# Hybrid encoder layer in fp32: one rotary pass for all queries, and a first pair of tiles multiplied before its tokens are normalised

## The chip, the cores and the metric

One core of a Trainium2 chip (trn2) runs the whole layer in one launch. The metric is device time in microseconds of one execution. The kernel before took 926.9 us, the median of three runs (925.67 to 927.23).

## What is computed

One encoder layer over 1024 tokens of width 1024, all in float32:

```
h = rms_norm(x, g_pre)
proj = h @ w_in                      # 1024 -> 7424 columns
a_b, a_c, a_x, a_z, b_q, b_k, b_v, b_z, m_q, m_z, gate_logits = split(proj)
ya = short_gated_conv(a_b, a_c, a_x, w_conv) * silu(a_z)
q, k = partial_rope(b_q), partial_rope(b_k)       # 8 query heads, 2 key heads of 64; the first 16 dims turn
yb = window_attention_with_sink(q, k, b_v, sink) * silu(b_z)
ym = memory_cross_attention(m_q, mk, mv) * silu(m_z)
merged = gates[0]*(ya @ w_up_a) + gates[1]*(yb @ w_up_b) + gates[2]*(ym @ w_up_m)
out = x + rms_norm(merged @ w_out, g_post)
```

The kernel works on transposed activations: channels on partitions, the 1024 tokens along a row. The rotary turn is `t*cos + swapped(t)*sin` over rows; with 16 of 64 rows turning, cos is 1 and sin is 0 in the others.

## The kernel before, in words

Each fp32 operand is split in a high and a low part of type fp32r, and a product is three matmuls: high x high, high x low, low x high. For a weight block ACT makes the high part (`high_part`, L1207) and POOL the low part (`low_part`, L766) in one of the 4 slots of `ring`; the slots are numbered in the order in which TensorE uses them. So each slot has a place on ACT, then on POOL, then on TensorE, and ACT and POOL take them in order between whatever else stands there.

The projection runs in pairs of 128-column tiles. The first three pairs (key, four query tiles, value) are direct: 96 matmuls of 128x512 a pair. From pair 3 (`P_DIRECT`) on, each pair is one level of Strassen-Winograd: seven products P1, P2, P6, P7, P4, P5, P3 of 12 matmuls each, on 512x512 blocks of h and their combinations T3, T2, T4, T1. Attention begins in pair 4: `scores(0)` stands on TensorE ahead of P6 of pair 4 (L977).

**Start.** SP loads four blocks of x (L502), the identity, weights and the other four blocks. ACT squares (L1217), DVE makes the inverse roots and scales x, TensorE transposes (`turn_x`, L953, four transposes for one chunk of 128 channels and 512 tokens), ACT makes the high part of a chunk from PSUM (L1228), DVE or POOL the low part (L1583, L776), DVE or ACT a copy (L1587, L1233). `first_pair` then does six matmuls a chunk for pair 0, sixteen chunks (0 to 7 are the first 512 tokens). TensorE fills the waits before with small matmuls (`warm`, L1085).

**Rotary.** For each of the key tile and the four query tiles DVE shuffles rows (L1707), multiplies by cos (L1717, which frees the PSUM bank: `cos_made`), by sin (L1721) and adds (L1723): four instructions of 128x1024. ACT then makes the high part (L1284), POOL the low part (L787), and SP stores both in DRAM (`store_rope`, L492 to L498). Between them DVE makes the combinations of h (L1594, L1599, L1607, L1612) and their low parts (L1617), and the sums of weights (L1626 to L1643). `load_block(0)` (L548 to L553) reads the first query and key blocks back before `scores(0)`. The order on every engine is written out by hand.

Of the kernel before, what the change touches and what calls it, by code (L numbers as in the profile page):

```python
# [7 lines left out]
P = 128  # L8
D = 1024
SEQ = 1024  # L10
KC = D // P
# [39 lines left out]
WARM_STEPS = (28, 8, 4)  # L51

ROOT_GROUPS = (slice(0, 2), slice(2, 4), slice(4, NB))

POOL_CHUNKS = (2, 6, 8, 10, 12, 14)
# [56 lines left out]
COS0, SIN0, SWAP0, QHI0, VR0, VP0 = 4096, 5120, 6144, 0, 12288, 12288  # L112
ROTATED = (7168, 2048, 7168, 2048, 3072)
SWAPS = (SWAP0, SWAP0, SWAP0, VP0 + SEQ, SWAP0)
# [35 lines left out]
ROPES = [(0, None), (1, 0), (2, 1), (3, 2), (4, 3)]  # L150
# [29 lines left out]
SWAP_ROWS = [(r + ROT // 2) % ROT if r < ROT else r for r in range(HEAD // 2)]  # L180

# [23 lines left out]
def hybrid_layer(nc, x, mem, w8, wup, wmem, wout, g_pre, g_mem, g_post, w_conv, sink,  # L205
                 cos, sin, mask, ident_in, out):
    ctx = ExitStack()
    with ctx:
# [17 lines left out]
        hc = sb("hc", [P, 7, 2, HC, HALF], F32R)  # L226
# [13 lines left out]
        q_d = dram("q_d", (NB, P, 2, GROUP, P))  # L240
# [22 lines left out]
        rope_high_at = [f32r(at, SEQ) for at in (QHI0, QHI0 + SEQ, QHI0, QHI0 + SEQ, SWAP0)]  # L263
        rope_low_at = [f32r(at, SEQ) for at in ROTATED]
# [41 lines left out]
        def rotated(j):  # L306
            return f32(ROTATED[j], SEQ)

        def swap(j):
            return f32(SWAPS[j], SEQ)  # L310

# [36 lines left out]
        def sig_block(n):  # L348
            return f32(SIG0 + n % 2 * HALF, HALF)

        x_landed = [sem(f"x_landed{b}") for b in range(NB)]
        ident_landed, small_landed = sem("ident_landed"), sem("small_landed")
        spot_landed = [sem(f"spot_landed{j}") for j in range(4)]
        rope_landed, swapped, roped = sem("rope_landed"), sem("swapped"), sem("roped")
        rope_hi, rope_lo = sem("rope_hi"), sem("rope_lo")
        rope_stored = [sem(f"rope_stored{j}") for j in range(len(ROPES))]
# [3 lines left out]
        xs_pool = sem("xs_pool")  # L360
        x_turned, h_copied, h_copied_act, comb_hi = sem("x_turned"), sem("h_copied"), sem("h_copied_act"), sem("comb_hi")
# [5 lines left out]
        sum_made = {T3: sem("t3_made"), T2: sem("t2_made"), T4: sem("t4_made"), T1: sem("t1_made")}  # L367
# [10 lines left out]
        mem_landed, mem_ssq, mem_var, mem_root, memx_ready = (sem("mem_landed"), sem("mem_ssq"), sem("mem_var"),  # L378
                                                              sem("mem_root"), sem("memx_ready"))
# [20 lines left out]
        sq_made, out_var, out_root, out_ready = sem("sq_made"), sem("out_var"), sem("out_root"), sem("out_ready")  # L400
# [24 lines left out]
        def wait_stored(eng, j):  # L425
            eng.wait_ge(rope_stored[j], 16 * (6 if ROPES[j][1] is None else 4))

# [32 lines left out]
        def _(sp):  # L460
# [62 lines left out]
            for j in range(4):  # L523
                load_spot(j, 2)
# [1755 lines left out]
```

## Time and profile before

| | |
|---|---|
| median of 3 runs | 926.9 us |
| the profiled execution: its own time, its span | 925.96 us, 924.1 us |
| TensorE busy | 907.8 us (98%) |
| VectorE, ScalarE, GpSimd busy | 657.1, 439.2, 453.4 us |
| DMA | 126.56 MB, 137 GB/s mean |
| granted TensorE clock | 0.996 of full speed |

A time in what follows is counted from the start of the span. An instruction's duration overlaps that of the next on its engine, so the pace of an engine is read from start to start.

### The profile page before, as it was taken

Reading aid. Unit: us, or ns where it says so; the run is one execution under the profiler, and the core shown is the slowest. Engines: PE = TensorE matmul, PEld = TensorE weight load, DVE = VectorE, ACT = ScalarE, POOL = GpSimd, SP = SyncE. Lnnn points to the kernel's source line nnn. Section 1 sums busy time; section 2 is a strip of 40 time slices with the busy share of each in tenths; the row PEclk is TensorE's granted clock in tenths of the full one; section 3 lists DMA queues with packets and bytes.
Section 4 is the critical chain, followed back from the end, with each engine's and each line's share of the span. In section 5 each row is a group of like instructions: output and inputs, shape, how many; then the busy total and the mean of one; then the engine's idle time right before and its main releaser. Section 6 shows DMA issues by size and latency. Waiting matters only on the chain.

```text
span 924.1 us, 12763 instructions
## 1 busy us (share of the span) xinstructions
PE 907.8 (98%) x4376; PEld 763.3 (83%) x4376; DVE 657.1 (71%) x1060; ACT 439.2 (48%) x849; POOL 453.4 (49%) x303
## 2 busy tenths in 40 slices
PE   9999999999999999999999999999999999999995
PEld 8788788888888888888888888888888888888784
DVE  5689976565656566656576178888797358899887
ACT  7624464444444466544463434343444544445341
POOL 3546844444444444444446744444443636668452
PEclk9999999999999999999999999999999999999998
DMA  7243846252525242525255322222222974750333
GB/s 287 96 116 83 228 144 210 90 171 91 170 91 169 96 128 102 193 91 171 108 174 174 116 80 80 79 78 82 80 69 68 333 262 143 258 181 0 142 110 137
DMA packets 82336, 126.56 MB, mean 137 GB/s; under 512 B 7136, under 2 KB 40544, under 8 KB 82272
## 3 DMA queue, kind: packets, MB, share of 16 engines
q1 hardware_dynamic: 81952, 125.61, 41.2%
q8 instruction: 36, 0.59, 0.2%
q14 instruction: 28, 0.23, 0.1%
q10 hardware_dynamic: 320, 0.13, 0.1%
HBM read 92.56 MB, written 33.55 MB: 136 GB/s over the span
## 4 chain that ended last, share of the span: by engine, by line
PE 81%; DVE 8%; ACT 3%; DMA 3%; POOL 2%; issue 2%; SPq 1%; DVEq 0%; ACTq 0%
PE pm L866 17%; PE pm L864 17%; PE pm L865 17%; PE pm L1162 3%; PE pm L1163 3%; PE pm L1161 3%; PE pv L999 2%; PE sa L987 2%; PE sa L1163 2%; PE sa L1162 2%; PE sa L1161 2%; PE pv L1078 2%; PE sa L1058 1%; DVE area L2158 1%; DVE area L2135 1%
## 5 line engine op out<-in xcount | busy, mean ns | idle before, releaser
L766 POOL TENSOR_TENSOR ring<-spots,ring 128x512 fp32r<-128x512 f32 x234 | 340.9, 1460 | 389.9 <-ACT ring L1207 377.9
L864 PE MATMUL pm<-hc,ring 128*128 128x512 f32 x784 | 308.6, 394 | 0.0
L866 PE MATMUL pm<-hc,ring 128*128 128x512 f32 x784 | 305.8, 390 | 0.0
L865 PE MATMUL pm<-hc,ring 128*128 128x512 f32 x784 | 305.5, 390 | 0.0
L1207 ACT ACTIVATE ring<-spots 128x512 fp32r<-128x512 f32 x234 | 146.2, 628 | 268.6 <-PE pm L866 177.5
L866 PEld LDWEIGHTS pm<-hc,ring 128*128 128x128 f32 x784 | 147.2, 188 | 31.2
L864 PEld LDWEIGHTS pm<-hc,ring 128*128 128x128 f32 x784 | 147.3, 188 | 29.3 <-issue 0.6
L865 PEld LDWEIGHTS pm<-hc,ring 128*128 128x128 f32 x784 | 147.4, 188 | 28.9
L1161 PE MATMUL pm<-hc,ring 128*128 128x512 f32 x128 | 49.9, 390 | 0.0
L1162 PE MATMUL pm<-hc,ring 128*128 128x512 f32 x128 | 49.8, 389 | 0.0
L1163 PE MATMUL pm<-hc,ring 128*128 128x512 f32 x128 | 49.8, 389 | 0.0
L766 POOL TENSOR_TENSOR ring<-area,ring 128x512 fp32r<-128x512 f32 x28 | 41.6, 1484 | 12.2 <-ACT ring L1207 11.1
L1826 DVE TENSOR_TENSOR area<-pv,area 64x512 f32<-64x512 f32 x16 | 11.0, 689 | 49.1 <-ACT area L1334 49.1
L1664 DVE TENSOR_TENSOR snaps<-pm,snaps 128x512 f32<-128x512 f32 x26 | 17.9, 690 | 37.9 <-PE pm L866 37.8
L1457 ACT ACTIVATE area<-area 128x1024 f32<-128x1024 f32 x24 | 25.4, 1057 | 38.0 <-DMA area<-raw_d 38.0
L1212 ACT COPY snaps<-pm 128x512 f32<-128x512 f32 x26 | 15.3, 588 | 45.9 <-PE pm L866 45.9
L1341 ACT ACTIVATE area<-area,st 128x384 f32<-128x384 f32 (+1 forms) x64 | 36.7, 574 | 0.0
L1676 DVE TENSOR_TENSOR area<-pm,snaps 128x512 f32<-128x512 f32 x26 | 17.9, 690 | 24.4 <-PE pm L866 24.2
L1658 DVE TENSOR_TENSOR snaps<-pm,snaps 128x512 f32<-128x512 f32 x26 | 18.0, 691 | 23.3 <-PE pm L866 23.3
L1653 DVE TENSOR_TENSOR area<-pm,snaps 128x512 f32<-128x512 f32 x26 | 18.0, 692 | 21.7 <-PE pm L866 17.3
L1349 ACT ACTIVATE area<-area,st 128x384 f32<-128x384 f32 (+1 forms) x64 | 32.5, 579 | 0.8 <-DVE st L1812 0.6
L1628 DVE TENSOR_TENSOR spots<-spots 128x512 f32<-128x512 f32 x26 | 30.6, 1176 | 0.9
(248 smaller groups left out, 1664.5 us busy)
## 6 DMA issues: line engine op xcount, KB each, us to landing
spots<-in_w SPq DMA_DIRECT2D x116, 256.0 KB, 3.2
raw_d<-area SPq DMA_DIRECT2D x72, 256.0 KB, 2.0
area<-raw_d SPq DMA_DIRECT2D x24, 512.0 KB, 4.4
area<-in_x SPq DMA_DIRECT2D x16, 512.0 KB, 4.2
spots<-in_wup SPq DMA_DIRECT2D x24, 256.0 KB, 4.5
spots<-in_wout SPq DMA_DIRECT2D x20, 256.0 KB, 3.7
q_d<-area_r SPq DMA_DIRECT2D x16, 256.0 KB, 4.3
area<-raw_d SPq DMA_DIRECT2D x16, 256.0 KB, 3.6
```

What stands on the lines that cost most here:

```text
L766: nc.gpsimd.tensor_tensor(ring_part(n, 1), operand(n), ring_part(n, 0).bitcast(F32), ALU.subtract).then_inc(lo_made, 1)
L864: pe.matmul(bank, hi, moving_hi(k), start=(k == 0), stop=False)
L865: pe.matmul(bank, hi, moving_lo(k), start=False, stop=False)
L866: mm = pe.matmul(bank, lo, moving_hi(k), start=False, stop=(k == HC - 1))
L1161: pe.matmul(dst, hi, y[:, at, 0, cols], start=(begin and c == chunks[0]), stop=False)
L1162: pe.matmul(dst, hi, y[:, at, 1, cols], start=False, stop=False)
L1163: mm = pe.matmul(dst, lo, y[:, at, 0, cols], start=False, stop=(end and c == chunks[-1]))
L1207: nc.scalar.activation(ring_part(n, 0), operand(n), ACT.Copy).then_inc(hi_made, 1)
L1341: ins = nc.scalar.activation(row, row, ACT.Exp, bias=st[:, 3, h:h + 1], accum_out=st[:, 5, h:h + 1])
L1349: ins = nc.scalar.activation(row, row, ACT.Copy, scale=st[:, 6, h:h + 1])
L1457: nc.scalar.activation(gate_of(g), gate_of(g), ACT.Sigmoid).then_inc(gate_sig, 1)
L1628: nc.vector.tensor_tensor(spots[:, A21, :], spots[:, A11, :], spots[:, A21, :], ALU.subtract).then_inc(s_made, 1)
```

## The change

First, the queries. ACT now copies each query tile out of PSUM (`copy_query`), SP copies its 2x16 turning rows into one tile (`gather`, at GATHER0), and DVE turns that tile once for all four (`swap_gathered`, `rotate(1)`), beside one turn for the keys. The rows that don't turn go from the copy to a high and a low part and to DRAM (`high_query`, `query_low_part`, `store_query`), the turned rows follow in two sets of eight small stores (`store_gathered`). Copies, key turn and gather live in the space of T4 and T3. `load_block(0)` waits for all of it, and loads the queries in one piece.

Second, the start. x's first four blocks land as two halves of columns and are transposed unscaled, so the first pair is multiplied with g_pre * x alone for tokens 0 to 511. Their inverse roots are spread over a PSUM bank as a row (`inverse_rows`, `spread_inverses`); DVE multiplies the eight chunks by it (`normalise`), ACT and DVE split them anew (`high_of_normal`, `low_of_normal`), and the products of the first pair, side 0 (keys) and side 1 (first queries), get the factor later (`scale_tables` for the keys' cos and sin, `scale_query`). In pair 1 the first side does its second half of tokens first (`second_side`).

```diff
-WARM_STEPS = (28, 8, 4)
+WARM_STEPS = 20
-POOL_CHUNKS = (2, 6, 8, 10, 12, 14)
+POOL_CHUNKS = (4, 6, 7, 10, 12, 14)
+TURNS_AT = {0: (), 1: (2, 3), 2: (4,), 3: (5,), 4: (6,), 5: (7,), 8: (9, 10), 9: (11,), 10: (12,), ...}
+SPREAD_BEFORE = 13
...
 SP
-            for b in range(4):
-                sp.dma_start(f32(X0 + b * D, D), x[b * P:(b + 1) * P, :]).then_inc(x_landed[b], 16)
+            load_spot(A11, 0)
             sp.dma_start(ident[:, :], ident_in).then_inc(ident_landed, 16)
             sp.dma_start(gpre[:, :], g_pre).then_inc(ident_landed, 16)
-            load_spot(A11, 0)
+            load_columns(0)
             load_spot(A21, 0)
...
+            load_columns(1)
             load_spot(A12, 0)
+            load_x(4)
             load_spot(A22, 0)
+            for b in range(5, NB):
+                load_x(b)
...
+            load_spot(A11, 3)
+            gather(1)
+            load_spot(A12, 3)
+            store_keys()
+            load_spot(A21, 3)
+            store_query(0)
+            load_spot(A22, 3)
+            gather(2)
+            store_query(1)
+            store_query(2)
+            gather(3)
+            store_query(3)
+            store_gathered(0)
...
 ACT
+            def copy_h(n):
+                if n not in POOL_CHUNKS:
+                    act.wait_ge(h_lo_dve, h_lo_count(n, h_lo_dve))
...
+                elif idx == T4:
+                    act.wait_ge(rope_lo, 1)
+                    act.wait_ge(query_lo, GROUP)
+                    for j in range(2):
+                        act.wait_ge(gathered[j], 64)
...
+            def high_query(c):
+                if c == 0:
+                    act.wait_ge(comb_dve, HC)
+                elif c == 1:
+                    act.wait_ge(rope_stored, 16 * 6)
+                else:
+                    wait_query_stored(act, c - 2)
...
 POOL
-            rope_low(0)
             low_part(8)
             low_part(9)
-            rope_low(1)
-            for n in range(10, 15):
-                low_part(n)
-            rope_low(2)
+            rope_low(0)
+            low_part(10)
+            query_low_part(0)
+            low_part(11)
+            query_low_part(1)
+            low_part(12)
+            query_low_part(2)
+            low_part(13)
+            query_low_part(3)
+            low_part(14)
             for j in (0, 2):
                 low_of_combination(T1, j)
             low_part(15)
-            low_part(16)
-            rope_low(3)
+            rope_low(1)
```

ACT in the first pair, before, chunks 14 and 15: a chunk is a high part (L1228) and a copy (L1233), and two weight blocks (L1207) stand between:

```order
L1228 ACTIVATE hc<-sa,gpre 128x512 [waits x_turned]
L1233 ACTIVATE area<-sa,gpre 128x512
L1207 ACTIVATE ring<-spots 128x512 [waits slot_done,spot_landed0]
L1207 ACTIVATE ring<-spots 128x512 [waits slot_done,spot_landed1]
L1228 ACTIVATE hc<-pv,gpre 128x512 [waits x_turned]
```

ACT now, chunks 8 to 10: squares (L1315) stand between, and a copy that waits for DVE's low part (L1333):

```order
L1326 ACTIVATE hc_r<-sa,gpre 128x512 [waits x_turned]
L1315 ACTIVATE hc_r,st<-area 128x1024 [waits x_landed1,x_landed0]
L1326 ACTIVATE hc_r<-sa,gpre 128x512 [waits x_turned]
L1333 ACTIVATE area<-sa,gpre 128x512 [waits h_lo_dve]
L1315 ACTIVATE hc_r,st<-area 128x1024 [waits x_landed1,x_landed0]
L1326 ACTIVATE hc_r<-sa,gpre 128x512 [waits x_turned]
L1333 ACTIVATE area<-sa,gpre 128x512 [waits h_lo_dve]
```

All copies of chunks moved to ACT, and from chunk 12 on the high parts of normalised chunks (L1341) too.

ACT around the high parts of T4, before. Slot 14 is the weight block of P6 of pair 3: the fourth L1207 row here after T4's four (L1241).

```order
L1284 ACTIVATE area_r<-area 128x1024 [waits roped]
L1207 ACTIVATE ring<-spots 128x512 [waits slot_done,spot_landed2]
L1241 ACTIVATE hc<-area 128x512 [waits t4_made] x4
L1207 ACTIVATE ring<-spots 128x512 [waits slot_done,spot_landed3]
L1207 ACTIVATE ring<-spots 128x512 [waits slot_done,spot_landed0]
L1207 ACTIVATE ring<-spots 128x512 [waits slot_done,spot_landed1]
L1207 ACTIVATE ring<-spots 128x512 [waits slot_done,s_made]
```

Now (L1412 is the high part of a query tile, L1353 that of T4, and the last row is slot 14):

```order
L1412 ACTIVATE area_r<-hc 128x1024 [waits n_made,query_copied,rope_stored]
L1304 ACTIVATE ring<-spots 128x512 [waits slot_done,spot_landed0]
L1412 ACTIVATE area_r<-hc 128x1024 [waits n_made,query_copied,query_stored0]
L1304 ACTIVATE ring<-spots 128x512 [waits slot_done,spot_landed1]
L1401 COPY hc<-pm 128x1024 [waits gathered1,query_lo,slot_done]
L1412 ACTIVATE area_r<-hc 128x1024 [waits n_made,query_copied,query_stored1]
L1353 ACTIVATE hc_r<-area 128x512 [waits gathered1,gathered0,t2_made,query_lo,rope_lo]
L1353 ACTIVATE hc_r<-area 128x512 [waits t2_made] x3
L1304 ACTIVATE ring<-spots 128x512 [waits slot_done,s_made]
```

Slot 14 stands behind four waits for stores or gathers to land, and T4 behind the last query tile.

DVE from T2's sums (L1753) over the keys' turn (L1861, L1863) to T2's low parts, now. These and the eight sums ahead of them read two SBUF operands each:

```order
L1753 TENSOR_TENSOR area<-area 128x512 [waits h_lo_pool,t3_made,t1_made]
L1753 TENSOR_TENSOR area<-area 128x512 [waits t3_made,t1_made] x3
L1861 TENSOR_TENSOR hc<-hc,snaps 128x1024
L1863 TENSOR_TENSOR hc<-hc 128x1024 [waits cos_made,dve_chain]
L1764 TENSOR_TENSOR hc_r<-area,hc_r 128x512 [waits comb_hi] x4
L1759 TENSOR_TENSOR area<-area 128x512 [waits n_lo,t2_made] x4
L1764 TENSOR_TENSOR hc_r<-area,hc_r 128x512 [waits comb_hi] x4
```

Before, two more rotary tiles (L1707, L1717, read from PSUM) stood among these.

## Rows read from the trace of the kernel before

**Rows 1.** Stretches of the span: busy time of each engine (instructions), clock, DMA

```profile
15.12:44.24 29.12, 28.26 (x144) 22.86 (x145) 19.75 (x30) 20.82 (x36) 17.80 (x12) 1.00 0.37 126
44.24:87.77 43.53, 43.53 (x194) 36.04 (x193) 39.39 (x47) 15.54 (x27) 22.16 (x12) 1.00 0.38 103
87.77:113.30 25.53, 25.53 (x117) 20.83 (x115) 25.05 (x27) 11.98 (x19) 22.90 (x13) 1.00 0.73 189
113.30:924.10 810.80, 797.32 (x3829) 670.92 (x3828) 566.79 (x943) 380.54 (x754) 387.44 (x262) 1.00 0.40 134
```

**Rows 2.** Waits of PE: us in total, times, longest

```profile
PE sa L977 <- DMA area_r<-kl_d: 1.5, 1, 1.5
```

**Rows 3.** Timeline of PE in the first pair: start, duration

```profile
35.03 0.48 PE L876 MATMUL pm<-hc,ring 128*128 128x512 f32 x1
...
36.86 0.48 PE L876 MATMUL pm<-hc,ring 128*128 128x512 f32 x1
...
40.16 0.39 PE L876 MATMUL pm<-hc,ring 128*128 128x512 f32 x1
...
41.52 0.39 PE L876 MATMUL pm<-hc,ring 128*128 128x512 f32 x1
```

**Rows 4.** Lines L502 and L473 (7.0 to 8.2 us): DMA issues, time to landing

```profile
L502 SPq DMA_DIRECT2D area<-in_x x4: 384/426/443, 0.7 to 2.1; - x4
DMA to landing us min/median/max: 3.4/5.2/6.9
L473 SPq DMA_DIRECT2D spots<-in_w x2: 472/482/493, 7.2 to 7.7; - x2
DMA to landing us min/median/max: 9.6/9.7/9.8
```

**Rows 5.** Timeline of ACT in the first pair

```profile
14.55 1.06 ACT L1217 ACTIVATE hc<-area 128x1024 fp32r<-128x1024 f32 x1
...
29.99 0.68 ACT L1233 ACTIVATE area<-sa,gpre 128x512 f32<-128x512 f32 x1
30.56 0.69 ACT L1228 ACTIVATE hc<-sa,gpre 128x512 fp32r<-128x512 f32 x1
```

**Rows 6.** Timeline of DVE

```profile
37.88 0.68 DVE L1599 TENSOR_TENSOR area<-area 128x512 f32<-128x512 f32 x1
...
42.50 1.78 DVE L1599 TENSOR_TENSOR area<-area 128x512 f32<-128x512 f32 x1
...
59.37 1.33 DVE L1707 STREAM_SHUFFLE area<-pm 128x1024 f32<-128x1024 f32 x1
...
71.51 4.90 DVE L1617 TENSOR_TENSOR hc<-area,hc 128x512 fp32r<-128x512 f32 x8
```

**Rows 7.** Timeline of POOL

```profile
28.13 1.29 POOL L776 TENSOR_TENSOR hc<-area,hc 128x512 fp32r<-128x512 f32 x1 [0.91 <-ACT area L1233]
...
72.85 7.22 POOL L766 TENSOR_TENSOR ring<-spots,ring 128x512 fp32r<-128x512 f32 x3 [3.82 <-ACT ring L1207]
...
93.16 3.97 POOL L766 TENSOR_TENSOR ring<-spots,ring 128x512 fp32r<-128x512 f32 x2
97.08 2.85 POOL L787 TENSOR_TENSOR area_r<-area,area_r 128x1024 fp32r<-128x1024 f32 x1
```

**Rows 8.** Timeline of SP's DMA issues

```profile
21.76 2.49 SPq L519 DMA_DIRECT2D kl_d<-in_sin  x4
...
58.92 0.49 SPq L492 DMA_DIRECT2D kh_d<-area_r  x1
```

**Rows 9.** DMA issues of the page: count, KB, us to landing

```profile
kl_d<-in_sin SPq DMA_DIRECT2D x4, 128.0 KB, 2.8
```

**Rows 10.** The chain that ended last, 60 to 115 us

```profile
63.60 4.26 DMA kl_d<-area_r
...
102.24 4.69 DMA q_d<-area_r
...
107.08 0.57 SPq L548
...
108.61 6.14 DMA area_r<-kl_d
```

More of the change, by code:

```diff
@@ L485, in store_rope, with store_query @@
-            def store_rope(j):
-                c = ROPES[j][1]
-                high, low, done = rope_high_at[j].bitcast(F32), rope_low_at[j].bitcast(F32), rope_stored[j]
-                sp.wait_ge(rope_lo, j + 1)
+                    at = g * HEAD + c * ROT
+                    sp.dma_start(f32(GATHER0, SEQ)[at:at + ROT, :],
+                                 query_raw[c][g * HEAD:g * HEAD + ROT, :]).then_inc(gathered[c % 2], 16)
+            def store_query(c):
+                sp.wait_ge(query_lo, c + 1)
+                for part, src in enumerate((query_high[c], query_low[c])):
+                    for g in range(2):
+                        to = ((1 - g) if part else g) * HEAD
+                        sp.dma_start(q_d[GROUP * g + c, to + ROT:to + HEAD, :],
+                                     src[g * HEAD + ROT:(g + 1) * HEAD, :].bitcast(F32)).then_inc(query_stored[c], 16)
@@ new lines, in store_gathered, with store_keys @@
+            def store_gathered(part):
+                sp.wait_ge((rope_hi, rope_lo)[part], 2)
+                src = (rope_high_at, rope_low_at)[part][1].bitcast(F32)
+                for g in range(2):
+                    to = ((1 - g) if part else g) * HEAD
+                    for c in range(GROUP):
+                        at = g * HEAD + c * ROT
+                        sp.dma_start(q_d[GROUP * g + c, to:to + ROT, :], src[at:at + ROT, :]).then_inc(rope_stored, 16)
+            def store_keys():
+                high, low = rope_high_at[0].bitcast(F32), rope_low_at[0].bitcast(F32)
+                sp.wait_ge(rope_lo, 1)
@@ L501, in _, with load_gathered_table @@
-            for b in range(4):
-                sp.dma_start(f32(X0 + b * D, D), x[b * P:(b + 1) * P, :]).then_inc(x_landed[b], 16)
+                    sp.dma_start(kh_d[own, g, :], high[own, :]).then_inc(rope_stored, 16)
+                    sp.dma_start(kh_d[other, g, :], high[own, :]).then_inc(rope_stored, 16)
+                    sp.dma_start(kl_d[own, g, :], low[own, :]).then_inc(rope_stored, 16)
+            def load_gathered_table(dst, src):
+                for n in range(HEADS):
+                    sp.dma_start(dst[n * ROT:(n + 1) * ROT, :], src[0:ROT, :]).then_inc(gathered_landed, 16)
@@ L1087, in _ @@
             pe.wait_ge(warm_made, 1)
[L1088 removed]
+            warm(WARM_STEPS)
             pe.wait_ge(ident_landed, 32)
[L1090 to L1096 removed]
+            turn_x(0)
+            turn_x(1)
             first_pair()
@@ L1744, in _ @@
-            sum_t1(HC - 1)
-            sum_t3(HC - 1)
+            inverse_rows()
+            low_of_h(11)
+            normalise(0)
+            normalise(1)
+            low_of_h(13)
+            for n in range(2, 5):
+                normalise(n)
+            low_of_h(15)
+            for n in range(5, KC):
+                normalise(n)
+            for n in range(HC):
+                low_of_normal(n)
+            scale_tables()
+            for n in range(HC, KC):
+                low_of_normal(n)
```

523 lines of the change are left out of this document (280 added, 243 removed).

## The prediction

> **What bounds the kernel now.** I read the stretches of the span first, then TensorE's waits, the chain that ended last, and the timelines of the five engines up to 115 us. TensorE has work all the time from 44.24 to 113.3 us, and 28.26 of 29.12 us in the first pair [rows 1]. Between 44 us and the attention its only wait is the one ahead of `scores(0)`, 1.5 us, for the key block that is read back from DRAM [rows 2]. So whatever is saved is TensorE's wait at the start plus this one, and whatever makes it wait anew is lost for good: from 113.3 us on the change alters nothing, and TensorE is busy for 797 of 811 us there [rows 1]. I therefore work out when `scores(0)` starts. Before, it starts 6.14 + 0.25 us after the issue at 108.61 [rows 10], at 115.0. A program change of under 0.2% (1.9 us) can't be told from none here.
>
> **The start.** The first product began at 15.12 us [rows 1]. x's four blocks (0.5 MB each, 2.1 MB) were issued from 0.7 us and landed from 4.1 to 9.0 (2.1 + 6.9); the last weight block, 5.3 MB in, landed at 7.7 + 9.8 = 17.5 [rows 4]. By this curve the first half columns (1.4 MB in) land at 6.9, A12 (2.95 MB) at 11.6 and A22 (3.7 MB) at 13.5. Behind 6.9 stand two turns (0.46 each, below), a high part of 0.69 [rows 5], a low part about as long and the steps from engine to engine; I take 2.7 us together: first product at 9.6, a **lead of 5.5 us**. The warm-up is shortened to end before that, and hides.
>
> **The first pair** takes 1.36 us a product, and 1.83 with a turn (41.52 - 40.16, 36.86 - 35.03) [rows 3], so 0.46 a turn. Now 14 turns and the spread follow the first product: 16 x 1.36 + 15 x 0.46 = 28.7 us; alone this would end at 38.3 instead of 44.24. But ACT can't feed it. Its pace is 0.57 us for each high part or copy from PSUM (30.56 - 29.99) and 1.1 for a square [rows 5]; it may go on to chunk 2 only when A12 has landed, and to chunk 3 with A22 (13.5). From there to the high part of chunk 15 stand 27 such passes (15.4), three squares (3.3), one scaling (1.0), two weight blocks, three normalised parts and two roots (2.9): 22.6 us. I add 4.8 for its own waits (the turn of chunk 8 behind all the scaling, about 2; DVE's rows of roots ahead of chunk 11's low part, 1.5; small ones), and get 40.9; low part and last product end at 43.5. So **the pair ends 0.7 us earlier, not 5.9**. Pairs 1 and 2 are four sides of 10.88 us (43.53 / 4) [rows 1]: pair 2 ends at 87.0 (before 87.77). Side 1 of pair 1 needs the keys' bank free: on DVE eight low parts at 0.60, two scaled tables, the scaled query, shuffle 1.24 and product 1.2 [rows 6], one POOL instruction in the way, end at 54.3 against 54.4 needed. I cost that at nothing; without the cover it is about 1.3 us for each further POOL instruction that gets in.
>
> **The port.** A two-operand DVE instruction of 512 takes 0.68 us alone and 1.78 beside POOL [rows 6]; POOL's takes 1.29 alone, and two take 3.97 beside DVE (1.98 each), a 1024 one 2.85 [rows 7]. Eight of DVE's ran undisturbed in 4.90 us from 71.51 [rows 6] while POOL, from 72.85, needed 7.22 for three [rows 7]: whoever waits is blocked, and the two times add. The Trainium skill, SBUF — State Buffer, section "SBUF: two separate sides", calls this pair of ports an exclusive lock held for a whole instruction; the trace agrees, and it speaks against this change, which puts long runs of such DVE work beside POOL's 1024-wide query parts.
>
> **Slot 14 and T4.** T4's high parts now wait for all four queries' low parts, and the queries pass through two buffers, so DRAM stores stand in the chain. From 54.3 on DVE: 12 sums at 0.60 (7.2), sin and add 2.4: 63.9. ACT's high part 1.1: 65.0. POOL's low part, 2.85 [rows 7]: 67.9. Six key stores, which took 8.9 us before from 58.92 [rows 8] to landing at 67.86 [rows 10]: 76.9. High and low part of query 1, 1.1 + 2.9: 80.9. Its four stores, 0.62 an issue [rows 8] and 4.7 to landing [rows 10], 6.6: 87.5. Query 3, 1.1 + 2.8: 91.4. T4's four high parts 2.2, slot 14's 0.6, POOL's 1.7: **95.9**. P6 of pair 3 wants it at 87.0 + 5.4 = 92.4: a new wait of 3.5 us.
>
> **P4.** Behind slot 14 POOL has T1's two, slot 15, the low part of the turned tile and slot 16: four at 1.98 and one at 2.85 [rows 7], 10.8 us, since DVE turns the gathered tile and makes T4's and T1's low parts (8 us of two-operand work) beside it. Slot 16 is ready at 106.7; P4 began at about 99.4 before (87.77, four products of 2.72, two sets of transposes). TensorE alone would reach `scores(0)` five products later, at 120.4.
>
> **The read back.** SP's load of A22 waits for slot 16 (106.7), then eight stores of 16 rows. No row shows such a store. Above it is bounded by the 128 KB one, 0.62 an issue [rows 8] and 2.8 to landing [rows 9]; below by the 0.38 us of the quickest x issue [rows 4] and nothing gained in landing. I take 0.5 and 2.8: 0.3 + 3.5 + 2.8 gives 113.3; three loads issued in 1.5 (107.08 to 108.61) and 6.14 + 0.25 [rows 10]: **121.3**. The ends are 120.4 (TensorE's own) and 122.1. A rule of the Trainium skill bears on these stores: SBUF — State Buffer, section "The DMA setup-cost knee", wants 128 partitions and large transfers. By its fit, an estimate, 64 KB would land in 2.15 us, and the sum would be 0.65 us less.
>
> **Sum.** 121.3 - 115.0 = +6.3 us on the profiled execution's 925.96: **932.3 us**. That execution lies 0.9 under the median of 926.9, which I don't add. Part by part: lead -5.5, lost again in the first pair +4.8, wait at P6 +3.5, further waits up to P4 +4.5 (together +7.3 there); the read back beyond TensorE's own +0.9; the old wait's 1.5 and its restart of 0.4 are in both times and come off once, -1.9. DVE loses 12 rotary instructions and 8 copies and gains 23 (8 products and 8 low parts of normalised chunks, 7 for rows, tables and query); beside the waits above they cost nothing, hidden under TensorE's four sides. The rest of the kernel is covered as before.
>
> **Rivals.**
> *The covers hold.* If the port costs little and a small transfer lands in about 2.3 us, T4 starts by 86, slot 14 is there by 90, and no wait is left, not even the old one: -0.7 - 1.5 - 0.4 (its restart): **923.4**. The point is T4's start: by 88 all is hidden. For it: each wait in my chain has been taken at its longer row. Against it: DVE was busy 39.4 of 43.5 us and 25.05 of 25.53 [rows 1]. 0.26.
> *A draw.* The port costs nothing but transfers land as in the rows: T4 starts at 88, only P4 (1.0) and the read back (2.2) wait, `scores(0)` at 115.8: **926.8**. 0.13.
> *DVE keeps the port.* As at 71.5, DVE's back-to-back run (T2's sums to T2's low parts, 20 instructions' worth of 0.60, 12 us) shuts POOL out from 60 to 72. Slot 8 is then 7 us late for pair 2, and the keys' store with it: `scores(0)` near 131, **942**. 0.08.
> *The lead survives.* ACT keeps up because weights land early, the first pair ends near 39: a further 4.5 off the first rival, **919**. 0.03. It would take a pace below every row of ACT.
> *The forecast,* slower by 3 to 11 us: 0.50.
>
> **How the numbers follow.** Range: the forecast's bounds for the port are two-sided. With T4 at 88 and half the loss after it I get 928; with T4's chain 4 us later than worked out, 937. The first rival joins below, so 922.5 to 937.5; DVE's long run and the surviving lead lie outside. Faster by over 0.2%: 0.26 + 0.03 less a little, 0.27. Within it: the draw, 0.14. Slower: 0.59.
>
> **What would show it.** In the new profile: first product near 9.6 us and the end of pair 0 near 43.5 (ACT without gaps from 14 to 22 us); TensorE waiting ahead of P6 of pair 3 for POOL's slot 14, ahead of P4 for T4's low part or slot 16, and ahead of `scores(0)` for the key block; DVE idle near 85 us for the gathered rows. Wrong would be: pair 0 ending before 41, no wait on TensorE between 44 and 112 us, or a wait in pair 1 for normalised low parts or in pair 2 for slot 8.

## The result and the profile after

| | before | changed |
|---|---|---|
| median (runs) | 927.07 us (4) | 934.97 us (4) |
| lowest to highest | 925.67 to 928.2 | 933.39 to 936.49 |
| ratio, 95% interval | | 1.0085 [1.0067, 1.0104] |
| profiled execution, its span | 925.96, 924.1 | 934.89, 933.1 |

The change makes the kernel 0.85% slower; the forecast was 932.3 us in a range of 922.5 to 937.5. Stretches of the changed kernel's span, cut at its first product, at the end of pair 0, at the start of pair 3 and at `scores(0)`, with the columns of [rows 1]:

```profile
11.95:47.11 35.16, 30.82 (x156) 23.85 (x157) 25.09 (x45) 27.86 (x50) 14.43 (x11) 1.00 0.45 164
47.11:90.63 43.52, 43.52 (x193) 36.04 (x192) 41.85 (x42) 19.02 (x27) 26.90 (x13) 1.00 0.54 150
90.63:123.16 32.53, 27.80 (x117) 22.04 (x116) 31.81 (x35) 15.66 (x26) 23.80 (x14) 0.95 0.58 164
123.16:933.10 809.94, 798.62 (x3829) 672.01 (x3827) 557.93 (x942) 379.97 (x751) 383.62 (x261) 1.00 0.40 133
```

`scores(0)` starts at 123.16 us instead of 115.0, 8.2 later; the rest is 0.8 longer than before (809.94 against 809.1). The first product is 3.2 us earlier (11.95 against 15.12), but the first pair takes 35.16 us instead of 29.12 [rows 1] and ends 2.9 us later. Pairs 1 and 2 take what they took, 43.52. From there to `scores(0)` it takes 32.53 instead of 27.2 (115.0 - 87.77), and the waits of TensorE say where:

```profile
PE pm L935 <- POOL ring L836: 4.7, 3, 3.1
PE pm L947 <- ACT hc_r L1326: 3.2, 3, 1.5
...
PE sa L1047 <- DVE area L1688: 1.2, 1, 1.2
```

The wait ahead of `scores(0)` [rows 2] is gone; in its place stand waits for the ring. Timeline of TensorE at P6 (slot 14), P7 (slot 15) and P4 (slot 16) of pair 3; the number in brackets is the idle time ahead of the instruction:

```profile
99.29 0.71 PE L935 MATMUL pm<-hc_r,ring 128*128 128x512 f32 x1 [3.06 <-POOL ring L836]
99.79 0.63 PE L936 MATMUL pm<-hc_r,ring 128*128 128x512 f32 x1
...
104.91 0.47 PE L935 MATMUL pm<-hc_r,ring 128*128 128x512 f32 x1 [0.16 <-POOL ring L836]
...
109.38 0.47 PE L935 MATMUL pm<-hc_r,ring 128*128 128x512 f32 x1 [1.51 <-POOL ring L836]
...
112.23 0.41 PE L935 MATMUL pm<-hc_r,ring 128*128 128x512 f32 x1
```

The last row is P5 (slot 17): it follows P4 with no wait. P6 runs at half the clock: the granted clock of 99 to 102 us is 0.56, and P6's twelve matmuls need 4.4 us (99.29 to 103.71) instead of 2.7. Counted on TensorE: 3.2 idle, 1.7 slow, 0.2 at the transposes and P7, 1.7 idle, less the old wait of 1.5: 5.3. That is the difference of the two stretches. What feeds it, first the high parts of T4 on ACT, then POOL:

```profile
94.08 2.19 ACT L1353 ACTIVATE hc_r<-area 128x512 fp32r<-128x512 f32 x4 [3.78 <-DMA area<-hc]
```

```profile
96.87 2.27 POOL L836 TENSOR_TENSOR ring<-spots,ring 128x512 fp32r<-128x512 f32 x1 [3.84 <-ACT ring L1304]
99.10 3.97 POOL L849 TENSOR_TENSOR hc_r<-area,hc_r 128x512 fp32r<-128x512 f32 x2
103.02 1.74 POOL L836 TENSOR_TENSOR ring<-spots,ring 128x512 fp32r<-128x512 f32 x1
104.72 2.85 POOL L854 TENSOR_TENSOR area_r<-area,area_r 128x1024 fp32r<-128x1024 f32 x1
107.53 6.38 POOL L836 TENSOR_TENSOR ring<-spots,ring 128x512 fp32r<-128x512 f32 x4
```

From 96.87 on POOL has no gap: slot 14, T1's two low parts, slot 15, the turned tile's low part, slot 16 (ready near 109.2). And DVE, whose run ahead of all this begins with the low parts of the normalised chunks (L1719); three products for tables and query stand between and behind them:

```profile
46.87 3.59 DVE L1719 TENSOR_TENSOR hc_r<-area,hc_r 128x512 fp32r<-128x512 f32 x4
...
51.69 2.50 DVE L1719 TENSOR_TENSOR hc_r<-area,hc_r 128x512 fp32r<-128x512 f32 x4
...
54.71 1.31 DVE L1848 STREAM_SHUFFLE hc<-pm 128x1024 f32<-128x1024 f32 x1
...
65.66 2.20 DVE L1863 TENSOR_TENSOR hc<-hc 128x1024 f32<-128x1024 f32 x1
67.79 6.88 DVE L1764 TENSOR_TENSOR hc_r<-area,hc_r 128x512 fp32r<-128x512 f32 x4
```

From 46.87 to 54.71, where the keys' shuffle starts, these take 7.8 us. The keys are turned at 67.86, 20.8 us after pair 0's end. Four low parts take 6.88 us there beside POOL, where eight took 4.90 undisturbed before [rows 6].

### The profile page after: what moved, and what is told of

The parts are those of the page before. It is cut to its first block, busy times and chain, and to the rows that moved or that the text cites. A ratio compares the mean times of both kernels' runs of the same rounds, so it can differ in the third digit from the quotient of the medians.

```text
span 933.1 us, 12775 instructions
## 1 busy us (share of the span) xinstructions
PE 909.5 (97%) x4340; PEld 762.3 (82%) x4340; DVE 657.6 (70%) x1062; ACT 446.4 (48%) x859; POOL 451.0 (48%) x303
## 4 chain that ended last, share of the span: by engine, by line
PE 84%; POOL 3%; DVE 3%; issue 1%; ACT 1%; DMA 1%; SPq 1%; DVEq 0%; ACTq 0%
PE pm L935 18%; PE pm L937 18%; PE pm L936 18%; PE pm L1259 3%; PE pm L1258 3%; PE pm L1260 3%; PE pv L1101 2%; PE sa L1089 2%; PE sa L1259 2%; PE sa L1258 2%; PE sa L1260 2%; PE pv L1180 2%; POOL ring L836 1%; PE sa L1160 1%; PE sa L935 1%
## 5 line engine op out<-in xcount | busy, mean ns | idle before, releaser
L935 PE MATMUL pm<-hc_r,ring 128*128 128x512 f32 x784 | 309.4, 395 | 4.7 <-POOL ring L836 4.7
L937 PE MATMUL pm<-hc_r,ring 128*128 128x512 f32 x784 | 306.3, 391 | 0.0
L936 PE MATMUL pm<-hc_r,ring 128*128 128x512 f32 x784 | 306.1, 390 | 0.0
L935 PEld LDWEIGHTS pm<-hc_r,ring 128*128 128x128 f32 x784 | 147.6, 188 | 35.0 <-issue 6.0
L937 PEld LDWEIGHTS pm<-hc_r,ring 128*128 128x128 f32 x784 | 147.6, 188 | 31.4
L936 PEld LDWEIGHTS pm<-hc_r,ring 128*128 128x128 f32 x784 | 147.8, 189 | 28.9
L1258 PE MATMUL pm<-hc_r,ring 128*128 128x512 f32 x128 | 49.9, 390 | 0.0
L1259 PE MATMUL pm<-hc_r,ring 128*128 128x512 f32 x128 | 49.8, 389 | 0.0
L1260 PE MATMUL pm<-hc_r,ring 128*128 128x512 f32 x128 | 49.8, 389 | 0.0
```

What stands on the lines that cost most here:

```text
L935: pe.matmul(bank, hi, moving_hi(k), start=(k == 0), stop=False)
L936: pe.matmul(bank, hi, moving_lo(k), start=False, stop=False)
L937: mm = pe.matmul(bank, lo, moving_hi(k), start=False, stop=(k == HC - 1))
L1258: pe.matmul(dst, hi, y[:, at, 0, cols], start=(begin and c == chunks[0]), stop=False)
L1259: pe.matmul(dst, hi, y[:, at, 1, cols], start=False, stop=False)
L1260: mm = pe.matmul(dst, lo, y[:, at, 0, cols], start=False, stop=(end and c == chunks[-1]))
```

## The experiments

The first product moves between 10.6 and 12.0 us from one profile of this start to the next, mostly with the landing of x. I read the profiles from two marks: pair 0's length (first product to its end) and the distance from pair 0's end to `scores(0)`. In the changed kernel these are 35.2 and 76.05 us.

**Half of the change alone.** The start of the kernel before, with the queries' half of the change:

```diff
-ROPES = [(0, None), (1, 0), (2, 1), (3, 2), (4, 3)]
+KHI0, QHI0 = 0, 2048
...
             load_spot(A12, 3)
-            store_rope(1)
+            store_keys()
             load_spot(A21, 3)
+            store_query(0)
             load_spot(A22, 3)
-            store_rope(2)
+            gather(2)
+            store_query(1)
+            store_query(2)
+            gather(3)
+            store_query(3)
+            store_gathered(0)
...
```

> The queries' half of the change alone: gathered rotary rows, the stores of 16 and 48 rows and all its orders, but x is scaled and turned at the start as in the kernel before (no unscaled tokens, no normalised chunks, no scaled tables). Theory A (TensorE starts pair 3 on time when DVE is free early: the loss of the whole change comes from DVE's work on normalised chunks, 16 instructions and tables, about 11 us, pushing keys, T4 and slot 16 back): pairs 1 and 2 end at 87.8 as before, query 3's tile is done at 77, T4's high parts start by 86, no wait ahead of P6 or P4, the wait of 1.5 us ahead of scores(0) gone: 924 to 925.5, about 2 us under the kernel before. Theory B (the queries' chain through two buffers and DRAM, with POOL's 1024-wide low parts, is late by itself): T4 still starts near 92, waits at P6 and P4 of 3 us or more together, 928 to 931.

Measured (queries_alone): 924.6 us (11 runs) against 926.22, ratio 0.9981 [0.9972, 0.999]: it beats both kernels. Stretches (first product to pair 0's end, then the next 43 us, which pairs 1 and 2 fill), ACT's start on T4, and TensorE at `scores(0)`, which has no wait ahead of it:

```profile
14.88:44.00 29.12, 28.26 (x145) 22.84 (x145) 19.76 (x30) 20.81 (x36) 17.74 (x12) 1.00 0.44 139
44.00:87.00 43.00, 43.00 (x191) 35.63 (x190) 37.04 (x33) 21.49 (x33) 26.00 (x14) 1.00 0.64 181
```

```profile
83.13 2.20 ACT L1290 ACTIVATE hc_r<-area 128x512 fp32r<-128x512 f32 x4 [3.55 <-DMA area<-hc]
```

```profile
112.44 0.39 PE L908 MATMUL pm<-hc_r,ring 128*128 128x512 f32 x1
112.66 0.39 PE L909 MATMUL pm<-hc_r,ring 128*128 128x512 f32 x1
112.89 0.28 PE L1021 MATMUL sa<-area_r 128*128 128x256 f32 x1
```

The distance from pair 0's end is 68.9 us, against 70.8 before and 76.05 with the whole change. Theory A's times hold: T4's high parts start 39.1 us after pair 0's end, in the changed kernel 47.0. So the queries' half gives 1.9 us, and all of the loss comes when the early start is added to it: 2.9 in the first pair and 7.2 behind it. (The start alone, with the rotary of before, wasn't built: the unscaled first query would need tables of its own. Its share is a difference, and holds beside the queries' half only.) That DVE's work is the reason, which theory A also says, this run doesn't show by itself; lows_narrow below tests it.

**Which of the three losses in pair 3 count.** Slot 14 ahead of T4 on ACT:

```diff
+            high_part(14)
             high_of_combination(T4)
-            high_part(14)
             high_of_combination(T1)
```

> The changed kernel with one exchange on ACT: slot 14's high part stands ahead of T4's four high parts. The profile of the change shows P6 waiting 3.06 us for slot 14 on POOL, then P6 at half the clock (0.43 us a matmul, about 1.7 us more), then P4 waiting 1.5 us for slot 16. Theory A (the three are one loss: P4 starts when POOL has made slot 16, and POOL runs without a gap from slot 14 to slot 16, so an earlier P6 only waits longer at P4): P6 starts near 96.3 and P4's wait grows to 3 to 5 us; slot 16 is earlier by the little that POOL starts earlier, 1 to 2 us: 933 to 934. Theory B (wait and clock are each on the path): all of 3.06 + 1.7 comes off, 930.

Measured (slot14_first): 934.04 us, ratio to before 1.0081 [1.0066, 1.0095]; the distance is 76.2, that is nothing gained.

```profile
103.46 0.77 PE L935 MATMUL pm<-hc_r,ring 128*128 128x512 f32 x1 [2.07 <-POOL ring L836]
...
108.45 0.47 PE L935 MATMUL pm<-hc_r,ring 128*128 128x512 f32 x1 [0.57 <-DVE hc_r L1764]
...
112.40 0.50 PE L935 MATMUL pm<-hc_r,ring 128*128 128x512 f32 x1 [0.97 <-DVE area L1800]
```

P6 has no wait any more (96.18), but P7 (103.46) waits for slot 15 and runs slowly, P4 (108.45) for T4's last low part, P5 (112.40) for a bank that DVE frees behind T4's and T1's low parts. The wait has moved to three other places. Theory A is right about the sum; it had named P4 alone.

The transposes in P6's wait:

```diff
+                if (p, name) == (P_DIRECT, "P6"):
+                    for _ in range(24):
+                        pe.transpose(bank_of(p, name)[:, 0:P], ident[:, :], ident[:, :])
```

> The changed kernel with 24 transposes of the identity into P6's own bank ahead of P6 of pair 3 (about 2.9 us of TensorE's work inside its wait of 3.06 us; the first product overwrites the bank). Theory A (the slow clock behind the wait costs nothing, since slot 16 on POOL sets P4's start): granted clock 1.0 at 99 to 102, P6's twelve matmuls in 2.7 us instead of 4.4, P4's wait grows from 1.5 to about 3.2, time within 0.5 of the changed kernel's 935. Theory B (the clock's 1.7 us is on the path): 933.3.

Measured (warm_in_wait): 934.53 us, 1.0086 [1.0073, 1.01], distance 76.2. The clock stays at 1.00, P6 begins at full rate, and the rest is waited for later (P6, P7 and P4):

```profile
99.81 0.47 PE L935 MATMUL pm<-hc_r,ring 128*128 128x512 f32 x1 [0.60 <-POOL ring L836]
...
105.41 0.47 PE L935 MATMUL pm<-hc_r,ring 128*128 128x512 f32 x1 [1.75 <-POOL ring L836]
...
109.89 0.47 PE L935 MATMUL pm<-hc_r,ring 128*128 128x512 f32 x1 [1.50 <-POOL ring L836]
```

Theory A: the slow P6 cost nothing, because the next slots were not there. Then the order itself, on POOL and, to feed it, on ACT:

```diff
             low_part(14)
-            for j in (0, 2):
-                low_of_combination(T1, j)
             low_part(15)
             rope_low(1)
-            for n in range(16, 20):
+            low_part(16)
+            for j in (0, 2):
+                low_of_combination(T1, j)
+            for n in range(17, 20):
                 low_part(n)
...
-            high_of_combination(T4)
             high_part(14)
-            high_of_combination(T1)
+            high_of_combination(T4)
             high_part(15)
+            high_part(16)
...
             rope_high(1)
+            high_of_combination(T1)
```

> The changed kernel with slot 14's high part ahead of T4's as in the run before it, and on POOL slot 15, the low part of the turned tile and slot 16 ahead of T1's two low parts (on ACT slots 15 and 16 ahead of the values' copy, T1's high parts behind the turned tile's high part). Theory A (POOL's queue in front of slot 16 sets P4): slot 16 is ready before T4's low parts, which DVE makes from 100.15 on, so P4 starts near 106 instead of 109.4 on T4's last low part, and the read back, 8 stores and 3 loads, stays covered: 931 to 932. Theory B (T4's chain, that is the gathered rows at 93.9 and DVE behind them, sets the end whatever POOL does): P4 starts near 108 to 109, 934 to 935.

Measured (slot16_early): 932.58 us, 1.0064 [1.0051, 1.0076]; distance 74.9. P4 starts 59.3 us after pair 0's end instead of 62.3, but only 1.15 of these 3.0 us arrive at `scores(0)`. TensorE at P4 and P5, the stretch of P4, and POOL behind slot 16:

```profile
105.16 0.77 PE L936 MATMUL pm<-hc_r,ring 128*128 128x512 f32 x1 [3.75 <-POOL ring L836]
...
109.80 0.47 PE L936 MATMUL pm<-hc_r,ring 128*128 128x512 f32 x1 [0.26 <-POOL ring L836]
```

```profile
105.00:108.00 3.00, 2.84 (x7) 2.29 (x8) 2.87 (x4) 0.63 (x1) 3.00 (x3) 0.50 0.86 274
```

```profile
104.98 3.42 POOL L849 TENSOR_TENSOR hc_r<-area,hc_r 128x512 fp32r<-128x512 f32 x2
108.35 5.06 POOL L836 TENSOR_TENSOR ring<-spots,ring 128x512 fp32r<-128x512 f32 x4
```

After 3.75 us idle P4 ran at 0.50 of the clock, and P5 began 4.6 us behind it. But P5 then still waited 0.26 us for slot 17, which POOL now makes behind T1's two low parts. A P4 at full rate would have waited for it longer, so the clock was not on the path here either: POOL's queue is, one slot further on. POOL's queue does set P4 too, and slot 16's low part, not T4's as I expected, still came last.

**DVE's added work.** The eight low parts of the normalised chunks, cut short:

```diff
-                nc.vector.tensor_tensor(hc[:, idx, 1, j, :], f32(place, HALF), hc[:, idx, 0, j, :].bitcast(F32),
+                nc.vector.tensor_tensor(hc[:, idx, 1, j, 0:8], f32(place, 8), hc[:, idx, 0, j, 0:8].bitcast(F32),
```

> Leaves out nearly all of the eight low parts of the normalised chunks: DVE makes 8 columns of 512 of each (0.60 us each before, 46.87 to 54.1 us; the run queries_alone, which has no such work, had T4's high parts at 83.1 us against 94.1). Theory A (DVE's added work in 45 to 60 us moves the keys' turn, the keys' store, the queries and T4 one for one, and slot 16 with them): 4 to 4.5 us off DVE, the keys' turn ends near 63.5 instead of 67.9, T4's high parts start at 89.5 to 90, slot 16 is ready near 104.8, P4 starts there, no wait or one under 1 us ahead of P6: 930 to 931. Theory B (the queries' own chain, ACT, POOL and stores behind tiles that TensorE finishes at 68.9 and 79.8, sets T4): T4's start stays within 1 us of 94, 934 to 935.

Measured (lows_narrow): 932.62 us, 1.0067 [1.0053, 1.0081]. T4's high parts start at 89.98, P4 at 105.35, both 4.1 to 4.2 us nearer to pair 0's end (47.19) than in the changed kernel, and the distance to `scores(0)` is 72.6, 3.4 less:

```profile
89.98 2.20 ACT L1353 ACTIVATE hc_r<-area 128x512 fp32r<-128x512 f32 x4 [4.01 <-DMA area<-hc]
```

```profile
99.31 0.60 PE L1062 MATMUL pv<-ident,area 128*128 128x128 f32 x4
100.87 0.47 PE L935 MATMUL pm<-hc_r,ring 128*128 128x512 f32 x1 [0.95 <-POOL ring L836]
...
105.35 0.47 PE L935 MATMUL pm<-hc_r,ring 128*128 128x512 f32 x1 [1.48 <-POOL ring L836]
```

Theory A: what is cut from DVE's work of 46 to 54 us moves the chain almost one for one (4.2 us at the keys' turn, at T4 and at P4; TensorE then waits 0.5 us for the key block). So this run shows 4.2 of the 7.9 us by which T4 starts later than in queries_alone, and 3.4 of the 7.2 in distance. The median fell by 2.4 only, the profiled execution (930.64) was the quickest of its five.

Could POOL, idle for 11 us, take some of it? (The first piece is POOL's list, the second DVE's.)

```diff
             low_part(7)
+            for n in range(5, KC):
+                low_of_normal(n)
             low_part(8)
...
             scale_tables()
-            for n in range(HC, KC):
-                low_of_normal(n)
+            low_of_normal(HC)
             scale_query()
```

> The changed kernel with three of the eight low parts of normalised chunks (5, 6 and 7) made by POOL behind slots 6 and 7, where POOL idles for 11 us (51.6 to 62.7), instead of by DVE (0.60 us each). Theory A (DVE's two-operand instructions and POOL's share a port and their times add): the three cost POOL 1.3 to 2 us each and stretch DVE's by as much, so that DVE saves 1.8 and loses 2 to 4: the keys' turn ends 0 to 2 us later than 67.86 and T4's high parts start at 94 to 96: 935 to 937. Theory B (the engines are independent, the low parts only had to leave DVE): the keys' turn ends 1.8 us earlier, 933.2.

Measured (three_lows_on_pool): 935.13 us, 1.009 [1.0074, 1.0106]; distance 76.1. DVE, then POOL:

```profile
53.31 1.72 DVE L1729 TENSOR_TENSOR hc_r<-area,hc_r 128x512 fp32r<-128x512 f32 x1
```

```profile
53.20 4.24 POOL L860 TENSOR_TENSOR hc_r<-area,hc_r 128x512 fp32r<-128x512 f32 x3
```

The one low part that DVE kept beside POOL took 1.72 us instead of 0.60. The keys' turn ended 20.0 us after pair 0's end instead of 20.75: of 1.8 us taken off DVE 0.75 were kept, and nothing of that at `scores(0)`. Neither theory in full: the times add where the two engines' instructions overlap, at one of DVE's low parts here. At `scores(0)` TensorE again waits for the key block, 0.30 us.

**The two buffers.** My forecast chained T4 through the stores:

```diff
-        query_high = [f32r((QHI0, KHI0)[c % 2], SEQ) for c in range(GROUP)]
+        query_at = (QHI0, KHI0, VR0, QHI0)
+        query_high = [f32r(query_at[c], SEQ) for c in range(GROUP)]
...
             store_query(1)
-            store_query(2)
             gather(3)
+            store_query(2)
             store_query(3)
...
```

> The changed kernel with a third buffer for the queries' high and low parts (query 2 in the free block behind T2, query 3 where query 0 was, so that query 3's high part no longer waits for query 1's store) and the gather of query 3 issued ahead of query 2's store. Theory A (DVE's lateness and POOL's queue set T4; the two buffers cost little): query 3's high part 1.5 to 2 us earlier but its low part not before POOL is free at 90.2, gathered rows landed near 89 instead of 93.9, T4 starts at 93.0 instead of 94.1, 934. Theory B (the stores through two buffers are what makes T4 late, as my forecast had it): T4 3 to 5 us earlier, 931.

Measured (third_buffer): 936.2 us, 1.0103 [1.0089, 1.0117]. T4 starts 46.0 us after pair 0's end instead of 47.0, as theory A says, but the distance is 77.6, 1.5 us longer:

```profile
108.74 0.66 PE L936 MATMUL pm<-hc_r,ring 128*128 128x512 f32 x1 [1.99 <-DVE hc_r L1768]
109.21 0.63 PE L937 MATMUL pm<-hc_r,ring 128*128 128x512 f32 x1
...
113.17 0.39 PE L936 MATMUL pm<-hc_r,ring 128*128 128x512 f32 x1
```

```profile
111.93 0.68 DVE L1804 TENSOR_TENSOR area<-pm,snaps 128x512 f32<-128x512 f32 x1
```

POOL's earlier slot 14 now falls beside DVE's turn of the gathered tile (its product by sin takes 2.29 us instead of 1.22), T4's low parts come later, and P4 waits for them. It still starts 62.2 us after pair 0's end, as in the changed kernel (62.3). What is lost comes between P4 and P5: 4.43 us (108.74 to 113.17) instead of 2.85 (109.38 to 112.23). P5 needs the bank that DVE frees behind its low parts (L1804, done at 112.61, here 66.1 us after pair 0's end), so with P4 at full rate P5 would still have come at about 66.1 instead of 65.1: some 1.0 us is DVE's lateness. The other 0.5 or so is the clock, since P4 ran at the lower level and P5 waited for nothing. In pair 3 this is the one run in which that level was on the path. I had forecast 934; the ranges of the two kernels' runs overlap, so the medians alone don't tell them apart.

**The first pair.** The three steps on DVE that refine the roots of x's blocks 4 to 7, left out:

```diff
+                if group == 0:
+                    nc.vector.reciprocal(st[:, 9, cols], st[:, 2, cols]).then_inc(inv_made, 1)
```

> Leaves out the three instructions that refine 1/root for x's blocks 4 to 7 (the reciprocal alone is kept). In the change's profile they are 23.09 to 25.68 on DVE (1.05, 0.16 and 1.31 us, two of them stretched beside POOL), ahead of the scaling, and TensorE then waits 1.16 us to turn chunk 8. Theory A (this chain holds the second half of the first pair): scaling starts 2.5 us earlier, the wait ahead of chunk 8's turn goes, pair 0 ends at 45.6 to 45.9 instead of 47.11, and since DVE works without a gap from 45 to 86 us everything behind moves with it: 1.2 to 1.5 us less, 933.5. Theory B (ACT's pace with two squares and nine copies sets the end of the pair whatever the roots do): the end stays within 0.4 us of 47.1, time 934.5 to 935.

Measured (root_unrefined): 935.72 us, 1.01 [1.0086, 1.0114]. What DVE saved, the port took back; DVE, then POOL:

```profile
24.91 0.18 DVE L1683 RECIPROCAL st<-st 128x4 f32<-128x4 f32 x1 [0.73 <-ACT st L1321]
25.12 3.94 DVE L1691 TENSOR_SCALAR area<-area,st 128x1024 f32<-128x1024 f32 x3
```

```profile
24.86 1.29 POOL L843 TENSOR_TENSOR hc_r<-area,hc_r 128x512 fp32r<-128x512 f32 x1 [2.06 <-ACT area L1333]
26.39 1.46 POOL L843 TENSOR_TENSOR hc_r<-area,hc_r 128x512 fp32r<-128x512 f32 x1 [0.25 <-ACT area L1333]
```

The three scalings take 3.94 us instead of 2.08, so from the root's arrival to chunk 8's turn it is 4.2 us instead of 5.0. And this execution began slow: TensorE idled 2.18 us ahead of the first turn and 1.47 ahead of the first product, and the granted clock was 0.50 from 12 to 15 us. Pair 0 took 36.4 us. The run doesn't settle its question.

```diff
+                width = 8 if b in (2, 3) else D
```

> Leaves out nearly all of two squares: ACT's squares of x's blocks 2 and 3 (1.06 us each, at 29.13 and 31.31 us, between the high parts of chunks 8, 9 and 10) take 8 columns instead of 1024. Theory A (ACT's pace sets the second half of the first pair): about 1.8 us come off ACT there, TensorE's wait of 1.38 us at 35.71 goes, and pair 0 ends 1.4 to 1.8 us earlier, near 45.5; time 933.3. Theory B (the spread of 1/root over the rows, that is DVE's squares of blocks 0 and 1 and its roots, holds the normalised chunks and with them ACT and TensorE): the end moves by under 0.5 us, 934.5 to 935.

Measured (squares_narrow): 934.24 us, 1.0085 [1.0071, 1.0098]. This profile also began slow (clock 0.60 from 11 to 14 us). From chunk 8's turn to the end of the pair it is 18.2 us (29.34 to 47.51) instead of 19.3 (27.85 to 47.11): 1.1 us off for 1.8 taken from ACT. ACT's pace is in the chain; ACT then waits 1.77 us for DVE behind its rows of roots (2.17 in the changed kernel), so DVE limits the rest.

```diff
-WARM_STEPS = 20
+WARM_STEPS = (24, 8)
...
             turn_x(1)
+            warm(WARM_STEPS[1])
```

> The changed kernel with the warm-up products of 128 columns raised from 20 to 24 calls ahead of the first turn and 8 more between the first two turns and the first product, where TensorE idled 1.5 us. In four of eight profiles of the changed kernel's start so far TensorE was idle up to 2.2 us ahead of the first turn and 1.5 ahead of the first product, and then ran the first 10 to 16 products' matmuls at a granted clock of 0.5 (0.43 us each instead of 0.23). Theory A (this costs about 2 us in those executions, since ACT and DVE follow the turns between the products): granted clock 1.0 from 9 to 17 us and a median of 933.3 to 934 instead of 935. Theory B (ACT's and DVE's chain in the first pair hides a slow start): 934.7 to 935.3.

Measured (warm_longer): 934.98 us, 1.0094 [1.0077, 1.0111]. The profile has the clock at 1.00 from 9 to 17 us, no idle time ahead of the first product, pair 0 in 35.0 us; but the median of six is that of the changed kernel. By the medians theory B.

```diff
+            load_columns(0)
             load_spot(A11, 0)
...
-            load_columns(0)
```

> As warm_longer, and x's first half columns (1 MB) are issued first of all, ahead of A11, the identity and the scales, which went ahead of them by 1.4 us. They landed 7.1 us behind their issue, at 8.0 to 9.3, where I had taken 6.9 from the curve of whole blocks. Theory A (a 1 MB transfer in rows of 2 KB shares the engines with all that is issued behind it and takes 7 us by itself): they land near 7.7, the first product moves by 1 us at most, and the second half of the pair, which waits for roots and squares over all blocks, does not move: within 0.7 us of warm_longer. Theory B (the order was the fault, and an earlier first product is kept to the end of the pair): 1.3 to 2 us under warm_longer.

Measured (columns_first): 933.93 us, 1.0085 [1.0069, 1.0102]. The half columns landed 5.1 us after an issue at 0.74, at 5.8, not at 7.7: in this one profile, the order made most of the difference. TensorE could not use it, since the longer warm-up ran to 9 us; the first product came at 11.42 and pair 0 ended at 46.91, between warm_longer's 46.12 and the changed kernel's 47.11. The 1.05 us under warm_longer is within both ranges of runs, so what an early landing is worth stays open.

**Both repairs.** The edits of warm_longer and slot16_early in one kernel:

```diff
-WARM_STEPS = 20
+WARM_STEPS = (24, 8)
...
-            for j in (0, 2):
-                low_of_combination(T1, j)
             low_part(15)
             rope_low(1)
-            for n in range(16, 20):
+            low_part(16)
+            for j in (0, 2):
+                low_of_combination(T1, j)
+            for n in range(17, 20):
...
```

> The changed kernel with the two repairs that the runs point to: warm_longer's warm-up, and slot16_early's order on ACT and POOL (slot 14 ahead of T4, slot 16 and the turned tile's low part ahead of T1's low parts). Theory A (both losses are separate: the start's clock, and POOL's queue ahead of slot 16, while DVE's added work of some 11 us and the first pair's later end stay): 930.5 to 931.5, still 4 us over the kernel before and 6 over queries_alone. Theory B (an order is all that was wrong with the change): 927 or less.

Measured (repaired): 933.75 us (932.51 to 935.55), 1.0073 [1.0057, 1.0088]: not better than slot16_early alone, and above its range. Its distance is 74.7, and P5 waits for slot 17 as in slot16_early. Its profiled execution also had a wait of 1.56 us for a slot at 846 us, and that of columns_first one of 1.71 at 848; the other twelve profiles have none there, and what brings it isn't shown. Neither theory holds: the time lies over theory A's 930.5 to 931.5, and the longer warm-up gave nothing beside the order, as it gave nothing alone.

## Why the prediction was right

The sign held, and so did the mechanism: POOL's slots 14 and 16 come late, and TensorE waits at P6 and P4. That the size came so near (934.97 measured for 932.3) is in part luck, since a first pair forecast too short and a read back forecast too long offset each other. By its steps:

- **The lead** was sized at 5.5 us and is 3.2. Half columns land 7.1 us behind the issue at 2.12, at 9.2, where I had put 6.9 from the curve of whole blocks [rows 4]; A12 and A22 come 1.7 us late (ACT takes them at 13.26 and 15.22, for 11.6 and 13.5). Why isn't shown: issued first of all they landed in 5.1 us (columns_first), and with the order unchanged in 6.3 (warm_longer). No run varied what is issued behind them by itself.
- **The first pair** was forecast to end at 43.5 and ends at 47.11: the step that was mis-sized most, by 3.6. I added 4.8 us for ACT's own waits. Of the 6.4 us that TensorE loses against 28.7, 2.0 are ahead of chunk 4's product (0.86, until POOL's low part was made) and ahead of chunk 8's turn (1.16). In the second one's chain DVE's steps on 128x4 numbers take 1.05 and 1.31 us beside POOL's low parts:

```profile
23.09 1.05 DVE L1655 SCALAR_TENSOR_TENSOR st<-st 128x4 f32<-128x4 f32 x1
24.18 0.16 DVE L1656 TENSOR_TENSOR st<-st 128x4 f32<-128x4 f32 x1
24.37 1.31 DVE L1657 SCALAR_TENSOR_TENSOR st<-st 128x4 f32<-128x4 f32 x1
```

  I had applied the port to long instructions alone. The Trainium skill, SBUF — State Buffer, section "SBUF: two separate sides", states that the lock is held for a whole instruction and that the other engine fully blocks. The trace agrees, for small instructions too: L1657 takes 0.16 us at 35.86, with POOL done, against 1.31 here.
- **Pairs 1 and 2**, four sides of 10.88: 43.52. The keys' bank was free at 57.2, needed at 58.0, and cost nothing, as forecast.
- **T4's start**: forecast 47.9 us after pair 0's end, measured 47.0. The chain was right in length. The stores through two buffers are in it as rows, but third_buffer shows that they decide little: with the third buffer T4 starts 0.9 us earlier, on POOL's low part of query 3.
- **P6**: 3.06 us for slot 14, forecast 3.5. **P4**: starts 18.75 us after pair 3's start (109.38 - 90.63), forecast 19.7 (106.7 - 87.0), for slot 16, which was named. Not foreseen: the clock. It cost nothing at P6 (warm_in_wait).
- **The read back** was forecast 0.9 beyond TensorE and is covered, by 1.4 us: the key block lands at 121.8 (116.80 + 5.0). The stores were priced right in sum. From slot 16 (109.2) to the first load's issue (115.70) it is 6.5 us, forecast 6.6; a 16-row store lands in 2.0 us in the median, but the last two, which the load waits for, take 2.6 and 2.7, where I took 2.8. The loads were priced too high: the third is issued 1.1 us behind the first, not 1.5, and lands in 5.0, not 6.14. By the fit in the Trainium skill, SBUF — State Buffer, section "The DMA setup-cost knee", 64 KB land in 2.15 us, an estimate; the trace agrees in the median and not for those last two.

```profile
L533 SPq DMA_DIRECT2D q_d<-area_r x16: 303/420/1061, 101.3 to 112.9; - x16
...
DMA to landing us min/median/max: 1.9/2.0/2.7
```

- **DVE's 23 added instructions** "beside the waits above cost nothing": true as counted, yet it hid the main thing. These instructions and the sums that slid behind them stand in front of the keys' turn, which ends 20.75 us after pair 0's end and in queries_alone 10.8; T4 starts at 47.0 and not 39.1. Eight of them, the low parts, are shown to make 4.2 us of that (lows_narrow); the rest is read from DVE's rows. I had the cause inside a chain and did not say what the chain would be without it.
- The errors: first pair +3.6, pair 3 and read back -1.8, the rest of the kernel +0.8; together 2.6, which is 934.89, the profiled execution, against 932.3.

None of the four rivals came. What "The covers hold" says of the stretch behind pair 0 (T4 by 86, no wait left) is what queries_alone does, with T4 at 83.13. Its 923.4 also lies near 924.6, but it counts 0.7 us for an early start that queries_alone hasn't.

## What to carry to other kernels

When a change has two halves, cost each alone before the sum: here one gains 1.9 us, the other added to it loses 10, and only the first was worth keeping. An early start is worth what arrives at the next full stretch of TensorE; if it is bought with work on the engine that prepares the stage after, count that engine's next 40 us. Several waits in a row for the same engine are one loss: look for the last instruction in its queue that they wait for, and price an edit there. And look at the slot behind it: slot16_early brought slot 16 forward by 3.0 us and met slot 17.

## What the runs showed of the chip that I had not expected

- TensorE's granted clock fell from the upper to the lower level (0.43 us between matmuls of 512 columns instead of 0.23) when TensorE took up work in pair 3 after idling 3.06 us (P6), 3.75 us (P4 in slot16_early), 2.63 us (P6 in three_lows_on_pool), 2.07 us behind another wait of 1.25 (P7 in slot14_first), and 2.01 and 1.99 us (P6 and P4 in third_buffer). After waits of 1.51 us (P4 of the changed kernel), 1.75 (P7 in warm_in_wait) and 1.48 (P4 in lows_narrow) it stayed. A product at the lower level lasted 1.6 us longer (P4 in third_buffer) to 2.5 (P6 in root_unrefined, all twelve matmuls slow).
- Waits alone don't tell it at the start. In slot14_first waits of 0.84 and 1.47 us, with eight transposes between, were followed by the lower level; in the changed kernel 0.74 and 1.48 were not. Five of the twelve experiments' profiles began with slow products. In these five pair 0 took 36.0 to 36.9 us, and in the others with this start 35.0 to 35.5. The 33 warm-up matmuls that are recorded took 4.6 to 4.9 us in the five and 5.3 to 6.0 in the changed kernel, slot16_early, third_buffer and lows_narrow, which have the same warm-up; what lies behind that isn't shown.
- What the lower level costs depends on what stands behind it: 0.5 us in third_buffer, where P5's bank was free 0.5 us before P4 was through, and nothing where the next slot was late (P6 of the changed kernel, P4 of slot16_early).
- An edit that brings one engine forward can delay DVE where the two meet: third_buffer had T4 0.9 us earlier and P5's bank free 1.0 us later.
- SP took 0.60 us to issue one store of the keys (L541) at 72.38 and 1.18 us for its twin of the other group at 74.89. DVE was in its back-to-back run at both times, and POOL was at work only at the first; what stretches it wasn't tried.
